# An expert layer's token rows: scattered once into a table in pass order and loaded plainly, in place of an indirect gather for each pass

## The reference

```python
logits = (xf @ w_router) + b_router            # 512 x 32
top_val, top_idx = lax.top_k(logits, 4)        # 4 experts of 32 for each token
gates = softmax(top_val)
def expert_block(xb, e):
    hu = xb @ w_up[e] + b_up[e]                # 1024 -> 2048
    x_glu = minimum(hu[:, :1024], 7.0)
    x_lin = clip(hu[:, 1024:], -7.0, 7.0)
    act = x_glu * sigmoid(1.702 * x_glu) * (x_lin + 1.0)
    return act @ w_down[e] + b_down[e]         # 1024 -> 1024
# each (token, expert) pair is computed, times its gate, summed per token
```

## Time and profile before

| what | us |
|---|---|
| median of 3 runs | 2961.04 |
| lowest and highest run | 2953.68, 2963.92 |
| the profiled execution's own time | 2956.22 |
| its span | 2954.6 |
| PE busy in the span | 2770.8 (94%) |
| VectorE busy | 1125.3 (38%) |
| GpSimd busy | 242.1 (8%) |

### The profile page before, as it was taken

One profiled execution on the slowest core, in us unless ns is written; L12 is line 12 of the kernel. 1 busy time (PEld: TensorE's weight loads), 2 busy tenths in 40 slices (PEclk: granted clock), 3 DMA queues, 4 the chain that ended last, 5 costly groups with the idle time before them and its releaser, 6 DMA issues.

```text
span 2954.6 us, 37476 instructions
## 1 busy us (share of the span) xinstructions
PE 2770.8 (94%) x15815; PEld 1366.1 (46%) x15815; DVE 1125.3 (38%) x1420; ACT 477.1 (16%) x936; POOL 242.1 (8%) x369
## 2 busy tenths in 40 slices
PE   7998989897889989898999999999999999999998
PEld 3445866332223323232333475467654334556763
DVE  3855454311111111111124253455436652444544
ACT  1113232000000000000001143000023662200001
POOL 1000011112111011110011500000000210000000
PEclk9988988999999999999999999999999999999999
DMA  9776235999999999999999131213132223321310
GB/s 340 286 257 255 74 115 191 385 345 416 384 394 408 409 404 408 407 413 397 413 407 350 9 127 52 86 57 114 57 80 59 66 50 114 107 86 57 114 57 29
DMA packets 172882, 648.23 MB, mean 219 GB/s; under 512 B 75965, under 2 KB 77573, under 8 KB 140305
## 3 DMA queue, kind: packets, MB, share of 16 engines
q1 hardware_dynamic: 156674, 607.76, 53.7%
q0 software_dynamic: 15984, 38.12, 4.1%
q10 hardware_dynamic: 64, 0.07, 0.0%
HBM read 626.43 MB, written 24.06 MB: 220 GB/s over the span
## 4 chain that ended last, share of the span: by engine, by line
PE 78%; DMA 12%; DVE 5%; ACT 2%; DVEq 1%; issue 1%; SPq 0%; ACTq 0%
PE ps L1867 14%; PE ps L2548 10%; PE ps L2583 10%; DMA slots<-in_w_down_dram 8%; PE ps L1905 8%; PE ps L2886 4%; PE ps L2619 4%; PE ps L2257 3%; PE ps L3142 2%; DMA slots<-in_ada_w_dram 2%; PE ps L1913 2%; PE ps L2513 2%; PE ps L2430 2%; PE ps L2533 2%; PE ps L1259 2%; DMA slots<-in_w_ada_dram 2%
## 5 line engine op out<-in xcount | busy, mean ns | idle before, releaser
L1867 PE MATMUL ps<-slots,hT 128*32 128x512 f32 x5120 | 563.2, 598 | 15.4 <-DMA slots<-in_w_up_dram 14.3
L1867 PEld LDWEIGHTS ps<-slots,hT 128*32 128x32 f32 x5120 | 165.5, 111 | 388.3 <-issue 362.6
L2583 PE MATMUL ps<-slots,work 128*128 128x512 f32 x672 | 289.6, 592 | 2.8 <-DVE work L2661 2.8
L1905 PE MATMUL ps<-slots,work 128*32 128x512 f32 x2112 | 247.8, 613 | 45.8 <-DMA slots<-in_w_down_dram 45.3
L2020 DVE TENSOR_SCALAR stage<-ps 128x512 f32<-128x512 f32 (+1 forms) x47 | 32.2, 686 | 549.0 <-PE ps L1871 548.6
L2583 PEld LDWEIGHTS ps<-slots,work 128*128 128x128 f32 x672 | 127.5, 190 | 162.5 <-issue 157.9
L2548 PE MATMUL ps<-hT,slots 128*128 128x256 f32 x768 | 168.7, 379 | 0.0
L1905 PEld LDWEIGHTS ps<-slots,work 128*32 128x32 f32 x2112 | 69.3, 112 | 194.5 <-issue 189.4
L2886 PE MATMUL ps<-hT,slots 128*128 128x512 f32 x352 | 156.8, 601 | 0.0
L2548 PEld LDWEIGHTS ps<-hT,slots 128*128 128x128 f32 x768 | 145.9, 190 | 22.4 <-issue 2.9
L2758 DVE TENSOR_TENSOR work<-work,ps 128x1024 f32<-128x1024 f32 x60 | 71.6, 1218 | 164.8 <-PE ps L2583 164.6
(11 more groups left out here) (610 smaller groups left out, 3447.7 us busy)
## 6 DMA issues: line engine op xcount, KB each, us to landing
slots<-in_w_up_dram SPq DMA_DIRECT2D x128, 2048.0 KB
slots<-in_w_down_dram SPq DMA_DIRECT2D x64, 2048.0 KB
slots<-in_mlp_w_dram SPq DMA_DIRECT2D x32, 2048.0 KB, 7.9
slots<-in_ada_w_dram SPq DMA_DIRECT2D x40, 1024.0 KB, 4.9
slots<-in_w_ada_dram SPq DMA_DIRECT2D x16, 1024.0 KB, 5.4
slots<-in_w_in_dram SPq DMA_DIRECT2D x5, 2048.0 KB
slots<-in_rnn_w_in_dram SPq DMA_DIRECT2D x24, 384.0 KB, 4.2
slots<-in_w_ada_dram SPq DMA_DIRECT2D x4, 2048.0 KB
```

The costliest lines, as they stand in the source:

```text
L1867: ins = pe.matmul(to, x[:, k, unit * UNIT:(unit + 1) * UNIT], upw[s][:, k % 2, col:col + CH], start=k == 0, stop=False)
L1905: ins = pe.matmul(to, actT[:, 4 * q + j, 64 * u + 32 * h:64 * u + 32 * h + 32], downw[sl[h]][:, j, half * CH:(half + 1) * CH], start=k == ...
L2583: ins = pe.matmul(ps[:, bank + t], x[:, k, t * P:(t + 1) * P], w[:, k], start=k == 0, stop=k == HK - 1)
```

## The change

`h2_dram` is still written (the overflow blocks gather from it), but the passes no longer read it. A new DRAM table `xs_dram` of 24 x 128 rows has the order of the passes' rooms. It is zero filled by four DMAs of 3 MiB. Once `slotf` is known, GpSimd scatters the rows of each tile, which now stay in four separate tiles (`h2_rows`: `stage`, `tmp` and two places in weight slots 2 and 3), straight into the table: 16 indirect DMAs of 128 rows of 4 KB, one for each tile and choice. Pairs without room have a slot number past the bound and are dropped. SP then loads each pass's rows by plain DMAs, 1 or 2 a pass, with 64 rows where a pass has only 32. `tok_of`, one half of `marks`, `xempty` and `xsl` are gone.

```diff
+        h2_rows = [stage[:], tmp[:], scratch0[:, 10240:11264], scratch0[:, 13312:14336]]
+        zero_row = scratch0[:, 12288:13312]
...
-                dst = (stage, tmp)[t % 2]
-                if t >= 2:
-                    v.wait_ge(S("stage_free"), TURNED + PIECE["2"] + t - 1)
-                    v.wait_ge(S("h2_out"), 16 * (t - 1))
-                pairs_of = dst[:].rearrange("p (j r q) -> p j r q", r=2, q=P)
+                pairs_of = h2_rows[t].rearrange("p (j r q) -> p j r q", r=2, q=P)
...
-                if t:
-                    sp.wait_ge(S("h2_out"), 16 * t)
-                sp.dma_start(h2_dram[t * P:(t + 1) * P], (stage, tmp)[t % 2][:]).then_inc(S("h2_out"), 16)
+                sp.dma_start(h2_dram[t * P:(t + 1) * P], h2_rows[t]).then_inc(S("h2_out"), 16)
...
+        XROWS = 24 * P
+        xs_dram = dram("xs_dram", (XROWS, D))
...
+        def xs_fill(g):
+            g.memset(zero_row, 0.0)
+            g.drain()
+            for q in range(4):
+                g.dma_start(xs_dram.rearrange("(p j) n -> p j n", p=P)[:, 6 * q:6 * q + 6], zero_row.unsqueeze(1).broadcast_to([P, 6, D])).then_inc(S("xs_out"), 16)
...
-            for at, n in ((0, D), (5120, 3 * D), (11264, D)):
-                g.memset(work[:, at:at + n], 0.0)
+            g.memset(xg[0], 0.0)
...
+            v.tensor_copy(xslot[:], slotf).then_inc(S("route_step"), 1)
...
-            for i in range(NPASS + 1):
+            def x_in(i):
+                if i >= 4:
+                    sp.wait_ge(S("xg_free"), i - 3)
+                first = 2 * UNIT * QBASE[RANKS[i]]
+                for tile, r0, n, ks in x_runs(i):
+                    sp.dma_start(tile[0:n], xs_dram[first + r0:first + r0 + n]).then_inc(S(f"xg_in{i % 4}"), 16)
+
+            e = expert(0)
+            for j in range(2):
+                load(sp, up_slot[0][j], moe_up_w(e, j), up_rows[up_slot[0][j]])
+            sp.wait_ge(S("xs_out"), 16 * (4 + TT * TOPK))
+            sp.wait_ge(S("h2_out"), 16 * TT)
+            x_in(0)
+            for j in range(2, 4):
+                load(sp, up_slot[0][j], moe_up_w(e, j), up_rows[up_slot[0][j]])
+            sp.wait_ge(S("route_step"), ROUTE["biases"])
+            x_in(1)
+            sp.wait_ge(S("route_step"), ROUTE["listed"])
+            x_in(2)
+            for i in range(1, NPASS + 1):
...
+                if i == 1:
+                    sp.wait_ge(S("route_step"), ROUTE["blocks"])
+                if i + 2 < NPASS:
+                    x_in(i + 2)
...
-        def moe_gather(g, i):
-            if i >= 4:
-                g.wait_ge(S("xg_free"), i - 3)
-            settle(g)
-            for q, units, at in quads(i):
-                n = units * UNIT
-                to = xg[i % 4][q * 64:q * 64 + n] if q < 2 else xg_rest[0:n]
-                g.indirect_dma_start(to, None, h2_dram, bass.IndirectOffsetOnAxis(ap=xsl[0:n, at:at + 1], axis=0),
-                                     bounds_check=T - 1, oob_is_err=False).then_inc(S(f"xg_in{i % 4}"), 16)
...
-            g.wait_ge(S("route_step"), ROUTE["rows"])
+            g.wait_ge(S("route_step"), ROUTE["slots"])
+            g.wait_ge(S("xs_out"), 16 * 4)
+            settle(g)
+            for t in range(TT):
+                for j in range(TOPK):
+                    g.indirect_dma_start(xs_dram, bass.IndirectOffsetOnAxis(ap=xslot[:, TOPK * t + j:TOPK * t + j + 1], axis=0), h2_rows[t], None,
+                                         bounds_check=XROWS - 1, oob_is_err=False).then_inc(S("xs_out"), 16)
...
-                if i + 4 < NPASS:
-                    moe_gather(g, i + 4)
```

More of the change, by code:

```diff
@@ L1272, in mix_pe @@
                 if t >= 2:
-                    piece_pe(pe, "2", t - 2, (stage, tmp)[t % 2], 4)
+                    piece_pe(pe, "2", t - 2, h2_rows[t - 2], 4)
             def logits(t):
@@ L1285, in mix_pe @@
             logits(0)
-            piece_pe(pe, "2", 2, stage, 4)
+            piece_pe(pe, "2", 2, h2_rows[2], 4)
             logits(1)
             logits(2)
-            piece_pe(pe, "2", 3, tmp, 4)
+            piece_pe(pe, "2", 3, h2_rows[3], 4)
             logits(3)
@@ L1424, in build @@
         N_ROUTE = 9 * 16
-        ROUTE = {name: n + 1 for n, name in enumerate(("maxima", "mask", "ranks", "table", "marks", "rows", "turned", "outs", "biases", "listed", "edges", "first", "blocks"))}
+        ROUTE = {name: n + 1 for n, name in enumerate(("maxima", "mask", "ranks", "table", "slots", "marks", "turned", "outs", "biases", "listed", "edges", "first", "blocks"))}
+        def xs_fill(g):
[3 more added lines that the diff above has]
+                g.dma_start(xs_dram.rearrange("(p j) n -> p j n", p=P)[:, 6 * q:6 * q + 6], zero_row.unsqueeze(1).broadcast_to([P, 6, D])).then_inc(S("xs_out"), 16)
         def route_fill(g):
@@ L1454, in route_pe @@
             for a in range(16):
-                ins = pe.matmul(ps[0:64, 4, 0:2 * NQ], in_row[:, a], marks[:, a].rearrange("p two q -> p (two q)"), start=a == 0, stop=a == 15)
+                ins = pe.matmul(ps[0:64, 4, 0:NQ], in_row[:, a], marks[:, a, 1], start=a == 0, stop=a == 15)
             ins.then_inc(S("route_product"), 1)
@@ L1555, in route_dve @@
             v.wait_ge(S("route_product"), TT + 4)
-            v.tensor_scalar(xempty, ps[0:64, 4, NQ:2 * NQ], 0.0, float(T), ALU.is_equal, ALU.mult)
-            v.drain()
-            v.tensor_tensor(xsl[:], ps[0:64, 4, 0:NQ], xempty, ALU.add).then_inc(S("route_step"), 1)
-            v.tensor_copy(dtab, ps[0:64, 4, NQ:2 * NQ]).then_inc(S("route_step"), 1)
+            v.tensor_copy(dtab, ps[0:64, 4, 0:NQ]).then_inc(S("route_step"), 1)
             v.wait_ge(S("route_product"), TT + 5)
@@ L1715, in moe_sp, with expert @@
             sp.wait_ge(S("route_step"), ROUTE["table"])
[L1716 removed]
+            def expert(i):
+                return sp.value_load(tab[0:1, RANKS[i]:RANKS[i] + 1], min_val=0, max_val=E - 1)
+            def x_in(i):
[17 more added lines that the diff above has]
+            for i in range(1, NPASS + 1):
                 if i < NPASS:
[L1718 removed]
+                    e = expert(i)
                     for j, s in enumerate(up_slot[i]):
                         load(sp, s, moe_up_w(e, j), up_rows[s])
[L1721 to L1724 removed]
+                if i == 1:
+                    sp.wait_ge(S("route_step"), ROUTE["blocks"])
+                if i + 2 < NPASS:
+                    x_in(i + 2)
+                e = expert(i - 1)
+                for j, s in enumerate(down_slot[i - 1]):
+                    load(sp, s, moe_down_w(e, j), down_rows[s])
             sp.wait_ge(S("route_step"), ROUTE["blocks"])
```

32 lines of the change are left out of this document (10 added, 22 removed).

## The result

The changed kernel takes **3001.8 us** (median of 4 runs, 2992.9 to 3005.1) beside 2960.4 us for the kernel before on the same chip (2953.7 to 2963.9): ratio 1.0138, 95% interval 1.0109 to 1.0166. The forecast was 2958 with a range up to 2976. The profiled execution has a span of 2991.2 us, against 2954.6.

A forecast was written before the change was run, and what follows sets the result against it. From about 645 us to the passes' end the weight stream sets the pace, TensorE close behind. Start +14.5 and stream -17.5 give -3.0 us against the profiled span of 2954.6; with the median 5 us above that, 2958 us, range 2938 to 2976.

The forecast's parts named there:

- Is the plain load free of this?: Expert passes after 645 us: plain loads lose 0.6 us per 64 rows, 0.9 per 96, nothing per 128; 17 us in all.
- Gathers cost 41 us beyond their bytes.: Expert passes after 645 us: 41 gathers each cost the DMA stream 1.0 us beyond their bytes.
- Padding adds 0.9 us.: Expert passes: padding three passes from 32 to 64 rows adds 0.4 MB, 0.9 us of DMA time.
- Three quarters reach the end.: Expert passes: of the 23 us net saved in DMA time, three quarters shorten the kernel.
- The stream's term: Expert passes after 645 us: replacing gathers by plain loads saves 17.5 us; bounds -5 and -30.
- The start, +14.5 us.: First expert pass: TensorE begins 13.5 us later, behind scatters and x load, plus 1 us for a lower clock.
- Rival (d): Before the passes: VectorE's casts and subtractions block GpSimd's descriptors, scatters come late, +9 us on the forecast, 2967 us; chance 0.11.
- Lateness of TensorE goes through to the end.: Pass of six units, 600 to 640 us: late DMA is forgiven up to some 7 us, late TensorE is not.
- rival (e): The start doesn't matter: lateness is forgiven at 600 to 640 us after all, -14 us, 2947 us; chance 0.07.
- Edits at nothing.: New table's zero fill (31 us, in a DMA gap), smaller VectorE and TensorE work, dropped waits: no effect on the time.
- (b): Expert passes: indirection causes the gathers' cost, plain loads run at full rate, all 41 us go, 2945 us; chance 0.24.
- (c): Slower: plain loads ahead of w_down cost 1.0 us for 64 rows, 1.7 for 96; +9.5 us, 2970 us; chance 0.16.

The follow-up runs named there:

- e9: Changed kernel with x loads of passes 4 and later spreading the same bytes over all 128 partitions, except the rest of passes over 128 rows: 2955.3 us, ratio 0.9979.
- e6: Changed kernel with its plain x loads issued by GpSimd on its own queue instead of SyncE, shapes unchanged: 2982.7 us, ratio 1.0086.
- e2: Changed kernel without the x loads of passes 4 and later: 2930.4 us, ratio 0.9891.
- e3: Kernel before the change, without the gathers of passes 4 and later: 2909.1 us, ratio 0.9817.
- e4: Changed kernel with VectorE's bias work held until the last scatter is issued, and two pass 1 weight loads sent earlier: 2997.0 us, ratio 1.0127.
- e8: Changed kernel with only the first 8 of 16 scatters issued and waited for: 2985.8 us, ratio 1.0087.
- e1: Changed kernel with every first x load of a pass widened to 128 rows: 2962.6 us, ratio 1.0005.
- e5: Kernel before the change, with gathers from pass 4 on widened to 128 rows, one filling both quads of a pass: 2936.0 us, ratio 0.9912.
- e10: Changed kernel with x loads issued by GpSimd and those of 64 and 96 rows widened to 128 rows: 2972.2 us, ratio 1.0025.

## Why the prediction was wrong

**The step that failed** is the price of the plain load beside a full stream, in "Is the plain load free of this?". From rows 10 I took 0.6 us lost for 64 rows, 0.9 for 96 and 17 us in all; the holes are 2.1 and 2.6 us in the mean, and the runs say 45 to 49 us. Rows 10 are a stretch in which such loads run among themselves, with nothing else waiting. They show how fast a narrow load is, and it is at half rate there, as said. They can't show what it does to others, and that is the larger part: the 64 rows would be done in 1.2 us at 218 GB/s, yet the stream loses some 2 us beyond their bytes. The stretch of rows 10 also holds loads into 96 and into 32 partitions, so its 218 GB/s is no check of the figure that the Trainium skill gives for partitions 0 to 63, as I had called it. The Trainium skill, which I had used for the partitions, has more on this: "DMA: Bandwidth & Descriptors", section "Back-pressure in remote DMA", says that a saturated SBUF port backs up to the DMA engines and stalls their other queues as well. It says so of transfers between cores; this case's trace agrees in kind (the DMA share at 1.00 while the rate falls to 340 GB/s), and by e9 the stall is gone when the same bytes reach all partitions. By that rule alone the queue wouldn't matter; here it does (e6, 1.2 us a load by the stage in place of 1.9).

In the terms of the sum:

- *Gathers cost 41 us beyond their bytes.* Right: 36 us by the medians, 38 by the stages.
- *Plain loads cost 17 us.* 49 us by the medians, 45 by the stages.
- *Padding adds 0.9 us.* The table moves 2.5 MB more, 5.8 us: I had counted the gathers' empty rows as fetched.
- *Three quarters reach the end.* More do: 54.6 us of stage for gathers that I priced at 41 and whose bytes are 16. The stream's term was -17.5 us; it is 71 - 52 = **+19** by the medians and +15.8 by the stages of before and after. This is 33 to 37 of the 44 us between 2958 and 3001.8.
- *The start, +14.5 us.* 19.1 us by the trace, 21 by e2 and e3: 5 to 7 us short. The 1 us for the clock in it is 0.6: from pass 0 to pass 2 it takes 51.4 us in place of 50.8. Rival (d) did occur: the slow scatters stand right in VectorE's long row of casts and subtractions, two of them end 0.13 us after a cast does (521.82 + 4.22 against 524.16 + 1.75), and in e4, without that work, none is slow. The rule of the Trainium skill in "SBUF — State Buffer", section "SBUF: two separate sides", holds here by the 2.13 to 4.23 us; whether casts or subtractions lock is not separated. But its price was too high, 2.8 us in place of 9. For the other 2 to 4 us the rate is the likely cause, 333 GB/s from 520 to 540 us in place of 411; no run tests it.
- *Lateness of TensorE goes through to the end.* For the most part, by e8: of 12.5 us at the start 9 arrive at the end of the stage; rival (e) is out.
- *TensorE's waits fall to about 45 us* of then 60: they rose to 69. The sign that I had named for a wrong forecast, a later part that shortens by less than 8 us, came true: from the begin of pass 2 to the overflow blocks it took 982.0 us in place of 966.8.
- *Edits at nothing.* The fill of the new table runs in the gap that was there before (from 420 to 440 us the engines move 406 GB/s in place of nothing), and nothing in e2 against e3 asks for a cost of it beyond the start.

**The rivals.** (b), indirection is the cause, is refuted twice: plain loads cost more, and wide gathers cost as little beyond their bytes as wide plain loads. (c) had the right mechanism and place, a plain load that costs like a gather, right ahead of the down weights, but it capped the price at the gather's; a plain load in SyncE's queue costs about twice that. No rival had both the price above the gather's and a start above 15 us, so the range ended at 2976. The evidence for its being wider was there: I had no row of a narrow load beside a saturated stream, called rows 10 the nearest, and then didn't ask what the neighbours of such a load lose.

## What to carry to other kernels

When a weight stream saturates the DMA engines, try to make every small transfer beside it reach all 128 partitions, even at the price of some useless rows: here 46 us came from nothing but spreading the same bytes (e9, which only measures, since its rows lie wrongly), 39 us from a usable form of it (e1), and 23 us in the kernel before from gathers of 128 rows, part of which may be their smaller number. Count the bytes too: a table with fixed rooms moves its empty rows, a gather with a bound skips them. Replacing indirect by plain transfers brought nothing by itself; ask first whether width, not indirection, is what shows as a dip. And price a transfer by what the stream beside it loses, in stretches around one that exists in that place, not by its own rate measured alone.

## What the runs showed of the hardware that I had not expected

- A plain load of 64 rows (256 KB) into partitions 0 to 63 takes some 2 us from the stream beyond its bytes on SyncE's queue with the weights behind it (1.6 to 2.6 over eleven loads), 1.2 us on GpSimd's queue, and an indirect gather of up to 64 rows 0.9 us.
- 96 rows cost no less than 64, though they reach more partitions: on SyncE's queue 2.6 us in the mean against 2.1, with ranges that overlap, on GpSimd's 1.4 both. Why is open.
- 128 rows cost little or nothing beyond their bytes, plain or indirect, on either queue (e1, e5, e10).
- Indirect scatters went out one every 1.27 us, and took up to 4.23 us each while VectorE ran casts and subtractions of 32x3072.
